# Six output-projection slabs of block one stream their columns in interleaved orders

## What is computed

```python
merged = g_a * (o_a @ w_up_dil[layer]) + g_b * (o_b @ w_up_sb[layer])
x = x + merged @ w_out[layer]
h2 = rmsnorm(x, norm_mlp_g[layer])
x = x + jnp.square(jax.nn.relu(h2 @ w_mlp_in[layer])) @ w_mlp_out[layer]
```

## Time and profile before

| what | us |
|---|---|
| median of 3 runs | 1407.74 (1407.22 to 1407.99) |
| span of the profiled execution, first to last instruction | 1405.3 |
| TensorE matmuls busy | 1397.8 |
| VectorE busy | 921.2 |
| ScalarE busy | 596.3 |
| GpSimd busy | 211.8 |
| the eight output-projection slabs | 368.08 to 412.70 |

### The profile page before, as it was taken

How to read it: one execution, slowest core, us unless ns; L and a number is a source line. 1 busy time by engine, 2 the same in 40 slices (tenths; PEclk the granted TensorE clock), 3 DMA queues, 4 the chain that set the end, 5 groups by cost and what they waited for, 6 DMA issues and landing times.

```text
span 1405.3 us, 21789 instructions
## 1 busy us (share of the span) xinstructions
PE 1397.8 (99%) x8746; PEld 1184.5 (84%) x8746; DVE 921.2 (66%) x1248; ACT 596.3 (42%) x842; POOL 211.8 (15%) x215
## 2 busy tenths in 40 slices
PE   9999999999999999999999999999999999999998
PEld 7898779777888989989888997778888998989886
DVE  6635433765767858577656778556756967758775
ACT  4324531553445434353244435344434535344353
POOL 4000000000022302211433020000022221302310
PEclk9999999999999999999999999999999999999999
DMA  5223123211336845635233322232225773927573
GB/s 183 90 91 113 61 68 102 72 31 59 100 99 169 188 133 144 157 114 153 91 96 99 92 63 82 64 103 90 90 90 139 180 162 113 214 91 191 138 175 109
DMA packets 154860, 161.61 MB, mean 115 GB/s; under 512 B 4010, under 2 KB 144660, under 8 KB 154788
## 3 DMA queue, kind: packets, MB, share of 16 engines
q1 hardware_dynamic: 122868, 129.12, 28.9%
q0 software_dynamic: 31904, 31.46, 12.3%
q10 hardware_dynamic: 16, 0.00, 0.0%
HBM read 157.68 MB, written 2.10 MB: 114 GB/s over the span
## 4 chain that ended last, share of the span: by engine, by line
PE 99%; ACT 0%; DVE 0%; issue 0%; POOL 0%; POOLq 0%; ACTq 0%
PE ps L2355 63%; PE ps L2420 17%; PE ps L2351 4%; PE ps L2377 4%; PE ps L2493 3%; PE ps L2748 1%; PE ps L2563 1%; PE ps L2777 1%; PE ps L2763 1%; PE ps L2867 1%; PE ps L2652 0%; PE ps L2695 0%; PE ps L2674 0%; PE ps L2949 0%; PE ps L2540 0%; PE ps L2713 0%
## 5 line engine op out<-in xcount | busy, mean ns | idle before, releaser
L2355 PE MATMUL ps<-AA,wh 128*128 128x512 f32 x1440 | 453.5, 396 | 0.0
L2355 PE MATMUL ps<-BB,wh 128*128 128x512 f32 x1088 | 342.2, 396 | 0.2 <-issue 0.2
L2355 PEld LDWEIGHTS ps<-AA,wh 128*128 128x128 f32 x1440 | 267.4, 188 | 62.6 <-DVE wl L1449 0.8
L2355 PE MATMUL ps<-AA,wl 128*128 128x512 f32 x720 | 283.4, 394 | 0.0
L915 ACT ACTIVATE wh<-raw 128x1024 fp32r<-128x1024 f32 (+2 forms) x149 | 141.5, 950 | 259.8 <-PE ps L2355 206.0
L2355 PEld LDWEIGHTS ps<-BB,wh 128*128 128x128 f32 x1088 | 202.2, 188 | 49.3 <-issue 1.6
L2355 PE MATMUL ps<-BB,wl 128*128 128x512 f32 x544 | 213.9, 393 | 0.0
L1449 DVE TENSOR_TENSOR wl<-raw,wh 128x1024 fp32r<-128x1024 f32 (+2 forms) x149 | 169.9, 1140 | 60.6 <-ACT wh L915 60.3
L2355 PEld LDWEIGHTS ps<-AA,wl 128*128 128x128 f32 x720 | 135.4, 188 | 30.9
L2355 PEld LDWEIGHTS ps<-BB,wl 128*128 128x128 f32 x544 | 102.3, 188 | 23.3
L2420 PE MATMUL ps<-Hl,wh 128*128 128x256 f32 x384 | 107.8, 281 | 0.0
(11 more groups left out here) (408 smaller groups left out, 2410.6 us busy)
## 6 DMA issues: line engine op xcount, KB each, us to landing
raw<-in_w_in SPq DMA_DIRECT2D x38, 1024.0 KB, 5.4
raw<-in_w_ff SPq DMA_DIRECT2D x31, 1024.0 KB, 5.4
raw<-in_w_mlp_in SPq DMA_DIRECT2D x16, 1024.0 KB, 5.4
raw<-in_w_mlp_out SPq DMA_DIRECT2D x16, 1024.0 KB, 5.3
zf<-in_w_mlp_out POOLq DMA_DIRECT2D x48, 256.0 KB, 4.8
zf<-in_w_ff POOLq DMA_DIRECT2D x48, 256.0 KB, 4.6
raw<-in_w_out SPq DMA_DIRECT2D x8, 1024.0 KB, 5.4
arena<-in_x SPq DMA_DIRECT2D x4, 512.0 KB, 7.1
```

Source lines behind the costliest of these rows:

```text
L2355: last = pe.matmul(dense_psum(t_ps, kind), a[:, k, :], b[:, o0 + k, col0:col0 + S1], start=start, stop=stop)
```

## The change

The six slabs T_OUT+1 to T_OUT+6 each get a form (streams, run). For form (h, r) both the moving operand and the output in the PSUM bank are described as `p b h r` instead of `p (h b r)`: the row of 512 columns is cut into h equal parts, and TensorE takes r neighbouring columns of the first part, r of the second, and so on through the h parts, and then the next r of each. Form (2, 64), for instance, takes columns 0 to 63, 256 to 319, 64 to 127, 320 to 383 and so on. The same order holds for operand and bank, so that each result column lands where it did. The first and the last slab of the projection, and all other slabs of the kernel, stay as they are.

```diff
         @block.tensor
         def _(pe):
-            def products(t_ps, slot, kt, Oh, Ol, o0, kind, k_from, k_to, ready=None, col0=0):
+            WALKS = {T_OUT + 1 + i: form for i, form in enumerate(
+                ((2, 64), (2, 32), (2, 16), (2, 8), (2, 2), (4, 16)))}
+
+            def walked(ap, form):
+                if form is None:
+                    return ap
+                streams, run = form
+                return ap.rearrange("p (h b r) -> p b h r", h=streams, r=run)
+
+            def products(t_ps, slot, kt, Oh, Ol, o0, kind, k_from, k_to, ready=None, col0=0, form=None):
...
-                            last = pe.matmul(dense_psum(t_ps, kind), a[:, k, :], b[:, o0 + k, col0:col0 + S1],
-                                             start=start, stop=stop)
+                            last = pe.matmul(walked(dense_psum(t_ps, kind), form), a[:, k, :],
+                                             walked(b[:, o0 + k, col0:col0 + S1], form), start=start, stop=stop)
...
-                products(t, t % 2, kt, Oh, Ol, o0, kind, 0, kt, ready, col0).then_inc(slab_done, 1)
+                products(t, t % 2, kt, Oh, Ol, o0, kind, 0, kt, ready, col0, WALKS.get(t)).then_inc(slab_done, 1)
```

## The result

| kernel | median us | runs | ratio to before, 95% |
|---|---|---|---|
| before | 1407.80 | 13 | |
| changed | 1410.67 (1409.87 to 1412.11) | 13 | 1.002 (1.0013 to 1.0027) |

A forecast was written before the change was run, and what follows sets the result against it. The prediction took TensorE's matmuls, busy 99% of the span, to bound the kernel. Its terms for instructions, description and column order summed as 0 + 0 + 0, so it forecast the unchanged median, 1407.7 us, range 1405.1 to 1413.0.

The forecast's parts named there:

- (a): Six edited slabs: the same 144 matmuls and weight loads, no wait, DMA or buffer added; cost 0.
- (b): Edited matmuls: taking up a description with more dimensions stays hidden behind the previous matmul's 231.6 ns; cost 0.
- Part (c), the read: Edited slabs: reading the moving operand in interleaved order was taken as 0, at most 4.9 us for 9648 steps.
- pace row: Transposes' start spacing: four with strided operands take 0.39 us, four contiguous 0.44, so strided loads aren't paced slower.
- duration row: Transposes' weight loads: 205 ns strided against 140 contiguous, 0.51 ns for each step that leaves the neighbour.
- Part (c), the write: Edited slabs: interleaved writing into the PSUM bank was taken as 0, with the read's high end standing for it.
- Low end: Edited slabs: removing the 18.3 ns excess over a column per tick in all 144 matmuls gains 2.63 us.
- R4: Edited slabs: interleaving removes part or all of the excess, at most -2.63 us, 1405.1 us; chance 0.05.
- R1: All six slabs: each step to a non-neighbour costs 0.51 ns, 4.9 us in all, 1412.6 us; chance 0.13.
- R2: Form (2, 2) slab only: two columns a place halve the rate, 5.0 us more, 1412.7 us; chance 0.12.
- R3: All six slabs: any interleaved write or read is slow, 30.0 us more, 1437.7 us; chance 0.07.
- R5: Edited slabs: the change doesn't do what it says, time as forecast; included in the 0.63 for no cost.

The follow-up runs named there:

- e2: Changed kernel with the six forms on the bank alone, the moving operand read plainly: all six slabs 5.56 us, one execution 1407.5 us.
- e7: Changed kernel with six other forms, mostly runs of two, on the bank alone, operand read plainly: slabs 5.56 or 5.57 us, one execution 1407.1 us.
- e9: Changed kernel with six other single-column orders on the moving operand alone, the bank written plainly: one execution 1405.3 us.
- e1: Changed kernel with the six forms on the moving operand alone, the bank written plainly: slab lengths of the changed kernel, one execution 1411.2 us.
- e6: Changed kernel with six forms of single columns, (256, 1) to (16, 1), on the moving operand alone, bank written plainly: one execution 1428.3 us.
- e4: Changed kernel with the slab of form (2, 2) walked plainly again: 1407.96 us, ratio to before 1.0006.
- e10: Kernel before with all eight output-projection slabs of block one reading the operand as two single-column streams, VectorE undoing the order: 1403.75 us, ratio 0.9976.

## Why the prediction was wrong

**The path** was read rightly: TensorE is the chain, each ns in these slabs came out at the end (slabs 3.04, medians 2.87 us), no other engine took part, and parts (a) and (b), instructions and taking up a longer description, cost 0: e2 and e7 have longer descriptions of the bank and took 5.56 us, and e9's operands have longer ones and took 5.18 or 5.56.

**Part (c), the read, is the step that failed.** It was put at 0 and cost 3.0 us, 2.35 of them in form (2, 2) (e1, e2). I took 0 by the pace row of the strided transposes over the duration row, and compared the 0.76 ns for each separated element with the 0.90 ns that form (2, 2) gives each pair. Three things were wrong with it. The 0.39 and 0.44 us aren't alike: after the strided four the next start is that of a 512-column matmul, after the contiguous four that of another transpose. The chain of the kernel before gives the strided four 0.47 us and the contiguous four 0.44, so by it they were paced slower, if only by 8 ns a transpose:

```profile
72.60 0.47 PE ps L2642 x4
132.33 0.44 PE ps L2674 x4
```

The row is of the weight side; on the moving side single columns four apart took 11.06 us a slab, 461 ns for 512, 0.90 ns each (e6). And the count was of places in the stream, while what counts is how many columns each of two phases takes from a group: in (2, 2) each phase changes group at every column, in plain order at every second. With that count the form isn't a walk of pairs at all for the read. The count gives the place of the loss, not its size: (2, 2) took 330 ns a matmul, (4, 2) 446.

**Part (c), the write,** taken at 0 for want of a row, was 0 (e2, e7). Of the two sentences of the Trainium skill, page Advanced Engine Details and Errata, section Memory Cachelines, that were set against each other for PSUM, the second holds here: pairs suffice. The first, that any non-contiguous pattern slows matmuls significantly, doesn't: twelve interleaved orders of the bank measured 5.56 or 5.57 us. Single columns were never written apart. The section's rule on SBUF asks for at least two hits on a 16-byte line, which is four float32 columns. The runs agree if it is counted for each phase: two hits 231.7 ns, one hit 432 to 461. But two hits aren't the full pace here; four took 215.8 ns.

**Low end.** The 18.3 ns of excess over a column per tick were read rightly, and R4's clause, nothing excludes that an order removes them, was right for an order that isn't among the six: 215.8 ns is 15.9 below plain. For the six forms it was wrong, none was below 5.56.

**The rivals.** R1 gave 4.9 us, in slabs of 0.1, 0.2, 0.4, 0.8, 3.1 and 0.4; measured 0.00, 0.12, 0.21, 0.27, 2.35 and 0.08. The rank is right but for (4, 16), and the cost isn't proportional to the steps: 0.18 ns a step for (2, 8), 0.38 for (2, 2), and (4, 16), with 0.03 us of its own (e4), pays a seventh of what (2, 16) does with as many. R2 named the slab, (2, 2), and put 5.0 us on it instead of 2.35; its reason for, that the plain stream isn't free already, was the telling one. What happened lies between the two: most in the shortest run, and a little in others. R2's limit of two columns a place isn't the one: single columns in form (2, 1) took 5.20 us (e6). R3 fell. R5 fell: the forms do act. What I named as what would show me wrong, a length that depends on h, showed too: (2, 16) 5.77 and (4, 16) 5.59 to 5.64, (2, 2) 7.91 and (4, 2) 10.71; for runs of two theory P gives the sense, for 16 it is open.

**The numbers.** 1410.67 lies in the range of 1405.1 to 1413.0, but the range had its high end from R1 and R2, whose prices of 4.9 and 5.0 us were too large by two thirds and for other mechanisms; that it held is in part luck. The forecast of no change, given 0.68 for within 0.2%, was the wrong case: the slowdown of 2.87 us is clear of noise, and just at the edge of what I had called no change. R2's own argument should have had more weight than a row from another port.

## What to carry to other kernels

Float32 moving operands (fp32r) in plain order don't stream at a column per tick: 231.7 ns for 512, 118.8 for 256. Read as two interleaved streams of single columns, by two rearranged dimensions in the operand's description, and put back by the reader of the bank, they take 215.8 and 113.0 ns, and this kernel, bound by TensorE, kept 49.2 of 56.5 us for the first and 10.7 of 11.7 for the second. Before taking a price from a row, ask whether it is of the same port, and whether what is counted (places in the stream) is what the time goes by. Only float32 operands of this kernel were tried.

## What was not expected of the hardware

- Of 512 float32 columns, a matmul takes 215.8 ns or 231.7 or 432 to 461, by how many columns in a row each of two interleaved phases gets from one group of four: 4, 2 or 1. The fastest is 213.3 ns, a column per tick of the 2.4 GHz clock, and 2.5 ns. By the Trainium skill, page TensorE: Matmul & The Clock Gate, section "Wait — 56ns, not 53.3ns?", that is the spacing of back-to-back matmuls at this clock. The woven order agrees with it at 512 columns (215.8 ns) and at 264 (112.5 ns, 110 and 2.5); at 256 it doesn't, 113.0 ns against 109.2, for a reason that is open. Plain float32 order doesn't agree at any of these lengths: 231.7, 122.2 (144 matmuls of 264 columns in 17.59 us of the chain before) and 118.8 ns.
- It doesn't matter where the two streams lie: 1, 4, 8, 128, 254, 255 or 256 columns apart all gave 5.18 to 5.20 us a slab.
- The bank takes runs of two and more columns in any of twelve orders, at no cost: 5.56 or 5.57 us a slab.
- VectorE reads a bank with step 2 in 692 ns, as it does in plain order (e10).
- Runs of 4 to 32 columns cost 0.03 to 1.1 us a slab in a pattern that none of the theories gives.
